# Products of zeros in TensorE's waits ahead of the first product of weights

## The reference, cut to what matters

```python
h = jnp.concatenate([meta, x], axis=1)
u = rms_norm(h, norm_mix_pre[l]) @ w_in[l]
u_sb, u_rw, gate_sb, gate_rw = jnp.split(u, cut, axis=-1)
...
merged = sigmoid(gate_sb) * (o_sb @ w_branch_sb) + sigmoid(gate_rw) * (o_rw @ w_branch_rw)
h = h + rms_norm(merged @ w_out, norm_mix_post)
f = rms_norm(h, norm_ffn_pre)
f = (silu(f @ w_ffn_gate) * (f @ w_ffn_up)) @ w_ffn_down
h = h + rms_norm(f, norm_ffn_post)
```

## Time and profile before

| | us |
|---|---|
| three runs | 890.24, 890.42, 892.93 |
| their median | 890.42 |
| the profiled execution's own time | 892.45 |
| its span | 890.6 |
| TensorE busy in the span | 874.9 |

### The profile page before, as it was taken

The page is one execution under the profiler, slowest core; times in us unless marked ns, Lnnn a source line. Parts: engine busy times, 40 slices in busy tenths (PEclk is TensorE's granted clock), DMA queues, the critical chain, the costliest instruction groups (busy, mean ns, idle before and its releaser), DMA issues.

```text
span 890.6 us, 19075 instructions
## 1 busy us (share of the span) xinstructions
PE 874.9 (98%) x8261; PEld 724.3 (81%) x8261; DVE 487.5 (55%) x644; ACT 412.6 (46%) x573; POOL 92.4 (10%) x92
## 2 busy tenths in 40 slices
PE   6999999999999999999999999999999999999997
PEld 5999999867787777767888898888888888888886
DVE  5459997346767656639575754444444444422333
ACT  6444666359788765555343642222222222211331
POOL 2015543111010101041100000000000000000000
PEclk9999999999999999999999999999999999999999
DMA  9322223311201121142267323333333333333321
GB/s 276 101 83 85 71 72 96 119 50 38 73 4 39 39 74 38 38 131 72 87 221 269 85 67 100 94 94 94 94 94 94 94 94 94 95 96 96 103 85 71
DMA packets 109008, 82.82 MB, mean 93 GB/s; under 512 B 2895, under 2 KB 99449, under 8 KB 108682
## 3 DMA queue, kind: packets, MB, share of 16 engines
q1 hardware_dynamic: 108938, 81.77, 30.3%
HBM read 75.99 MB, written 5.77 MB: 92 GB/s over the span
## 4 chain that ended last, share of the span: by engine, by line
PE 93%; DVE 5%; issue 1%; ACT 1%; DMA 0%; DVEq 0%; SPq 0%
PE psum L576 47%; PE psum L1850 18%; PE psum L1601 9%; PE psum L1638 6%; PE psum L1775 2%; PE psum L1893 2%; PE psum L1494 2%; PE psum L1785 1%; DVE w_lo L566 1%; PE psum L1756 1%; PE psum L1804 1%; DVE shift_diff L1168 1%; PE psum L1485 1%; DVE k_mod L1209 1%; DVE v_t L1173 1%
## 5 line engine op out<-in xcount | busy, mean ns | idle before, releaser
L576 PE MATMUL psum<-h_hi,w_hi 128*128 128x512 f32 (+1 forms) x736 | 230.7, 349 | 0.8 <-DVE w_lo L566 0.8
L576 PE MATMUL psum<-h_lo,w_hi 128*128 128x512 f32 (+1 forms) x736 | 229.7, 347 | 0.0
L576 PE MATMUL psum<-h_hi,w_lo 128*128 128x512 f32 (+1 forms) x736 | 228.7, 346 | 0.0
L566 DVE TENSOR_TENSOR w_lo<-w_raw,w_hi 128x1024 fp32r<-128x1024 f32 x69 | 88.3, 1280 | 113.3 <-ACT w_hi L561 109.0
L576 PEld LDWEIGHTS psum<-h_hi,w_hi 128*128 128x128 f32 x736 | 127.8, 188 | 22.3 <-issue 1.9
L576 PEld LDWEIGHTS psum<-h_lo,w_hi 128*128 128x128 f32 x736 | 127.7, 188 | 18.5 <-issue 0.5
L576 PEld LDWEIGHTS psum<-h_hi,w_lo 128*128 128x128 f32 x736 | 127.8, 188 | 17.7
L1080 ACT ACTIVATE w_hi<-w_raw 128x1024 fp32r<-128x1024 f32 x44 | 46.7, 1062 | 171.6 <-PE psum L576 164.4
L1440 DVE TENSOR_TENSOR w_lo<-w_raw,w_hi 128x1024 fp32r<-128x1024 f32 x44 | 53.9, 1226 | 130.6 <-ACT w_hi L1080 126.4
L561 ACT ACTIVATE w_hi<-w_raw 128x1024 fp32r<-128x1024 f32 x70 | 73.8, 1056 | 77.2 <-PE psum L1850 55.8
L1850 PE MATMUL psum<-w_hi,act_hi 128*128 128x512 f32 x144 | 45.7, 390 | 0.0
(11 more groups left out here) (304 smaller groups left out, 1538.0 us busy)
## 6 DMA issues: line engine op xcount, KB each, us to landing
w_raw<-in_w_in SPq DMA_DIRECT2D x42, 512.0 KB, 4.0
w_raw<-in_w_g SPq DMA_DIRECT2D x22, 512.0 KB, 3.8
w_raw<-in_w_u SPq DMA_DIRECT2D x22, 512.0 KB, 3.9
w_raw<-in_w_d SPq DMA_DIRECT2D x22, 512.0 KB, 3.5
w_raw<-in_w_out SPq DMA_DIRECT2D x8, 512.0 KB, 5.2
kept_gates<-gate_raw SPq DMA_DIRECT2D x10, 256.0 KB, 2.9
sig_t<-kept_gates SPq DMA_DIRECT2D x10, 256.0 KB, 3.0
x_in<-in_x SPq DMA_DIRECT2D x4, 512.0 KB, 7.3
```

The lines of the kernel that those rows point to most:

```text
L566: nc.vector.tensor_sub(lo[:], raw[u % RAW][:], hi[:].bitcast(F32)).then_inc(w_split, 1)
L576: mm = nc.tensor.matmul(o, w[:, (w0 + i) * P:(w0 + i + 1) * P], xs[:, k, c0:c1], start=(n == 0), stop=(n == total - 1))
```

## The change

VectorE sets 256 columns of `kT` to zero at the start. TensorE multiplies a 128x128 piece of these zeros with another, in float32, into bank 1 of PSUM, where nothing reads it: six times behind the norm row, twice between the transpositions of the second and the third block, and five times between those of the third block and the first product of weights. Nothing is removed.

```diff
+        idle_ok = sem("idle_ok")
...
             v_.memset(ones, 1.0).then_inc(ones_ok, 1)
+            v_.memset(kT[:, 0, 0:2 * P], 0.0).then_inc(idle_ok, 1)
...
+            def keep_busy(n):
+
+                for _ in range(n):
+                    t_.matmul(psum[:, 1, 0:P], kT[:, 0, 0:P], kT[:, 0, P:2 * P], start=True, stop=True)
+
+            pe.wait_ge(idle_ok, 1)
             pe.wait_ge(gain_in, 16)
             pe.wait_ge(ones_ok, 1)
             for h in range(2):
                 mm = t_.matmul(bank(2 + h), ones, xn[3][0:1, 512 * h:512 * h + 512], start=True, stop=True)
             mm.then_inc(gain_pe, 1)
+            keep_busy(6)
             pe.wait_ge(ident_in, 16)
-            for i in range(3):
-                block_transpose(i)
+            block_transpose(0)
+            block_transpose(1)
+            keep_busy(2)
+            block_transpose(2)
+            keep_busy(5)
             pe.wait_ge(w_split, 1)
             pe.wait_ge(n_lo, 5)
             unit_part(0, range(0, 4), bank(0, HALF), 0, HALF)
```

## The result

| | before | after |
|---|---|---|
| median of 13 runs, us | 892.54 | 894.02 |
| lowest and highest, us | 890.24, 893.28 | 893.18, 895.39 |
| profiled execution, us | 892.45 | 894.28 |
| its span, us | 890.6 | 892.5 |

A forecast was written before the change was run, and what follows sets the result against it. TensorE, busy 874.9 of 890.6 us, was taken as the bound. The earlier runs' median of 890.42 us less the 1.9 us clock gain gave 888.5, rounded up to 888.6 us; range 887.4 to 891.4 us.

The forecast's parts named there:

- The bound, and the most a high clock can give: At the start: TensorE bounds the kernel; a high clock from 15.42 us on begins unit 1 1.90 us earlier.
- The price of the zeros: Products of zeros before the first product of weights: 0.21 us a piece, costing 0 or, at low clock, 1.5 us.
- Does the clock come up: Behind the norm row: the six extend unbroken work to 6.1 us, lifting the clock for the full 1.90 us.
- The likeliest case: Clock high before the first product of weights: full gain of 1.9 us, 888.5 us, chance 0.55.
- the first rival: Clock rises only in the last five, near 16.3 us: gain 0.75 us, 889.7 us, chance 0.2.
- Behind this point TensorE is the bound, and I carry the gain to the end in full.: From unit 1 to the end: TensorE, 98% busy, keeps the whole 1.90 us won at the start.
- The executions timed are not like the one profiled: Kernel before: in fast runs the clock may already rise earlier than 19.7 us, leaving little gain; 890.2 us, chance 0.1.
- The case of a loss: At the last five: zeros do nothing for the clock, first product 1.5 us late; 891.2 to 891.9 us, chance 0.15.
- Theory A: From the experiments: 52 added instructions move code-block borders, one into small products, its fetch behind a store and a load.

The follow-up runs named there:

- e2: Kernel after, with the fifth gate's store and the next load held until TensorE finished the fifth head's cumulative sums; 891.50 us, 0.9994 of the kernel before.
- e3: Kernel after, with the same columns of zeros in 5 wide products instead of 13 (20 added instructions, not 52); 1.0002 of the kernel before.
- e4: Kernel after without the six and the two products of zeros, only the last five left; 0.9995 of the kernel before.
- f3: Kernel after without the two products between, and with the fifth gate's store and the next load held; 0.9998 of the kernel before.
- f4: Kernel after with ones in place of zeros, and the fifth gate's store and the next load held; 891.96 us, 1.0000 of the kernel before.
- g1: Repeat of f2 (only the last five products, store and load held), whose profile was a disturbed one; 890.50 us, 0.9983 of the kernel before.
- g2: Kernel after with only the last five, made as two wide products (8 added instructions), no transfers held; 0.9995 of the kernel before.
- g3: Same as g2, with the fifth gate's store and the next load held; 0.9998 of the kernel before.
- e1: Kernel before plus thirteen tiny 32x32 float32 products of zeros behind the norm row, 52 added instructions; 895.68 us, 1.0036 of the kernel before.
- f1: Kernel before with only the fifth gate's store and the next load held, no products of zeros; 0.9996 of the kernel before.
- g4: Kernel after with only the six products behind the norm row, and the store and load held; 891.25 us, 0.9989 of the kernel before.
- f2: Kernel after with only the last five products, and the fifth gate's store and the next load held; 890.54 us, 0.9983 of the kernel before.

## Why the prediction was wrong

- *The bound, and the most a high clock can give.* Right. 1.90 us were worked out; e2, in whose profile the clock rose ahead of everything, has transpositions 3 and 4 at 17.34 and 19.31, where 17.36 and 19.35 were replayed. VectorE's `w_lo` is the next limit, as said.
- *The price of the zeros.* Right in size: 0.21 us a piece, six hidden but for 0.12 us (transposition 0 starts at 9.46 and not 9.34, which delays nothing behind it), the two at the low level 0.8 us late, and the first product late by what the five then overrun, 0.5 us because the clock rose among them.
- *Does the clock come up.* The six didn't lift it in the execution profiled; it rose 0.24 us into the last five. The likeliest case was taken wrongly, and the first rival came, at 1.3 us rather than 0.75, because the clock rose at 15.0 and not at 16.3 us. Of the profiles with the last five, all show the clock up by 15.7 us (after, e2, e3, e4, f3, f4, g1, g2, g3), of those without them none before 19 us (before, e1, f1, g4); of five with the six and the five, two show it before 10 us. But the rise can't be put down to the five in each case: in f4, g1 and g3 it came at 14.4, 13.4 and 13.4 us, before the five began, and in g1 and g3 before any product of zeros. What is shown is that with the five it was never later than 15.7 us.
- *"Behind this point TensorE is the bound, and I carry the gain to the end in full."* This is the step that failed. It priced the added instructions by their time, and not by their place in the stream. The 52 instructions put a border of code at a bad place: a hole of 2.57 us and 3.4 us at the low clock behind it, 3.8 us in all, of which 0.5 us come back around the border at 317 us, against 1.3 us won. e1 shows it with the instructions alone.
- *The executions timed are not like the one profiled.* Partly right: the first three runs of the kernel before misled by 2 us. Thirty-two later ones spread from 889.7 to 894.0 us, more than any effect measured here; what makes that spread is not settled. In g1 and g3 the clock rose at about 13.4 us, in transposition 2, ahead of any product of zeros and after the same work as in the kernel before, where it did not rise until 19.7. So the same work doesn't always lift it at the same time, and this is probably part of the spread: the 22 executions of f2 and g1, with the five, lie between 890.0 and 891.2 us.
- *The case of a loss* gave 891.2 to 891.9 us by a clock that never rose. The sign came true by another mechanism, so its chance was no credit to it.

What a border costs can be added up from the traces, and this also explains the holes that stay when nothing is held back. TensorE passes a border; the packet for the next one comes some time later; the first product behind that next border starts 2.2 to 2.7 us after the packet, in each of the 25 cases. When the 256 instructions between the two borders run shorter than these two times together, the difference is the hole. At record 8,130, in us:

| kernel | border ahead to packet | data moved meanwhile, KB | packet to first product | the 256 instructions ran | hole |
|---|---|---|---|---|---|
| before | 2.26 | 533 | 2.24 | 4.26 | 0.23 |
| after | 2.27 | 601 | 2.50 | 2.20 | 2.57 |
| e2 | 0.56 | none | 2.37 | 2.21 | 0.72 |
| e4 | 2.39 | 600 | 2.40 | 3.84 | 0.95 |
| g1 | 0.60 | none | 2.86 | 3.44 | none |

So the packet stood behind the store and the load before the change too. What the 52 instructions changed is which 256 instructions lie ahead of the border: 4.26 us of work, with eight wide products of the attention and four of 512 columns in it, became 2.20 us, 64x64 products alone. Theory A had the right place and the right queue, but not this half of it. Left open: why the packet comes as late as 0.3 to 1.1 us behind the border where no data move, and why a packet needs 2.2 to 2.7 us to be of use.

## What to carry to other kernels

In a long stream without a loop, an edit anywhere moves all code behind it. Before a small gain at one end is believed or a small loss blamed on the edit, look in the trace for holes of the engine in the middle of a row of equal instructions, with "issue" as their releaser; a kernel with the same number of instructions and none of the work tells code from work. Keep large transfers out of stretches in which TensorE runs many small products: a wait on the queue that issues them cost nothing here, where their data are needed late (f1, 0.9996). Filling a wait to lift the clock paid here just ahead of the work that should run fast: with the five the clock was up by 15.7 us in nine profiles of nine, while the six alone left it low until 19.6 us in the one that was profiled.

## What the runs showed of the hardware that was not expected

- TensorE's block of code stood behind a store and a load of 768 KB together: it came at 294.1 us with them and at 291.9 without, in a kernel that was 0.5 us ahead at that place, so 1.7 us later.
- After holes of 2.57 and 2.92 us (after, e1) the clock was granted at 1.2 GHz for 3.4 us, beginning 1.8 and 1.3 us after TensorE had resumed; after holes of up to 1.26 us (f3) it was not.
- A block of 256 instructions of 64x64 float32 products ran in 2.2 us, less than the 2.9 us from the border ahead to the first product of the next block, with no data moving (e2).
- The Trainium skill ("TensorE: Matmul & The Clock Gate", Part 4: PE-mode transpose) says that the high clock doesn't engage for transpositions. Here it rose in the midst of them (g1, 0.21 to 0.11 us apart at 13.4 us, with only the norm row and transpositions ahead; e2 at 9.8 us) and stayed up through the sixteen that followed in e2.
